# A mixture of experts in 4 chunks of 896 inner columns in place of 7 of 512

## The reference

```python
def moe_swiglu(h, w_router, w_gate, w_up, w_down):
    logits = (hf @ w_router).astype(jnp.float32)
    top_val, top_idx = lax.top_k(logits, TOP_K)      # 2 of 8
    gates = jax.nn.softmax(top_val, axis=-1)
    ...
    def expert_block(args):
        xb, e = args
        return (jax.nn.silu(xb @ w_gate[e]) * (xb @ w_up[e])) @ w_down[e]
    ...
    out = jnp.einsum('tk,tkd->td', gates.astype(y.dtype), y)
```

## Time and profile before

| | us |
|---|---|
| median of 3 runs | 2171.3 (2170.34 to 2173.81) |
| the profiled execution, its own time | 2171.86 |
| its span in the profile | 2170.1 |
| PE busy in the span | 2023.1 |
| DVE busy | 1515.5 |
| ACT busy | 1197.9 |

### The profile page before, as it was taken

The page is one execution under the profiler, slowest core; times in us unless marked ns, Lnnn a source line. Parts: engine busy times, 40 slices in busy tenths (PEclk is TensorE's granted clock), DMA queues, the critical chain, the costliest instruction groups (busy, mean ns, idle before and its releaser), DMA issues.

```text
span 2170.1 us, 22855 instructions
## 1 busy us (share of the span) xinstructions
PE 2023.1 (93%) x9571; PEld 1664.5 (77%) x9571; DVE 1515.5 (70%) x1370; ACT 1197.9 (55%) x1151; POOL 148.7 (7%) x118
## 2 busy tenths in 40 slices
PE   5999998999988799989769999999999999999995
PEld 4877776888977588867548788888888888888884
DVE  4645454444697544467558878887988888798886
ACT  5554344343643433344237667676776767677772
POOL 1301100000141200031010000000000000000000
PEclk9999998999999899989669999999999999999998
DMA  7434334444522444533139989899999989899992
GB/s 259 155 117 155 114 120 176 174 155 175 187 85 97 175 179 162 183 136 117 39 106 339 361 324 362 326 371 332 362 359 330 364 323 369 322 358 367 341 360 93
DMA packets 217661, 511.55 MB, mean 236 GB/s; under 512 B 4318, under 2 KB 8528, under 8 KB 217552
## 3 DMA queue, kind: packets, MB, share of 16 engines
q1 hardware_dynamic: 215232, 502.81, 64.3%
q0 software_dynamic: 1424, 4.59, 0.7%
q10 hardware_dynamic: 896, 2.62, 0.3%
HBM read 508.95 MB, written 1.05 MB: 235 GB/s over the span
## 4 chain that ended last, share of the span: by engine, by line
PE 85%; DVE 7%; ACT 3%; DMA 3%; issue 1%; POOL 0%; DVEq 0%; ACTq 0%; POOLq 0%
PE PS L373 25%; PE PS L374 25%; PE PS L375 25%; DVE WLB L1472 1%; DMA ring<-in_moe_w_down 1%; PE PS L846 1%; ACT WHB L994 1%; PE PS L379 1%; PE PS L393 1%; PE PS L708 1%; PE PS L798 1%; DMA ring<-in_w_mem_kv 1%; PE PS L481 1%; DVE WLX L1472 1%; DVE AR L1813 1%
## 5 line engine op out<-in xcount | busy, mean ns | idle before, releaser
L1472 DVE TENSOR_TENSOR WLB<-ring,WHB 128x2048 fp32r<-128x2048 f32 (+1 forms) x356 | 660.8, 1869 | 190.5 <-ACT WHB L994 190.2
L994 ACT ACTIVATE WHB<-ring 128x2048 fp32r<-128x2048 f32 (+1 forms) x356 | 546.4, 1540 | 408.1 <-PE PS L375 360.6
L1472 DVE TENSOR_TENSOR WLX<-ring,WHX 128x2048 fp32r<-128x2048 f32 (+1 forms) x204 | 455.3, 2244 | 76.1 <-ACT WHX L994 76.1
L994 ACT ACTIVATE WHX<-ring 128x2048 fp32r<-128x2048 f32 (+1 forms) x204 | 383.2, 1883 | 226.8 <-PE PS L375 178.9
L373 PE MATMUL PS<-WHB,XH 128*128 128x512 f32 (+1 forms) x688 | 279.3, 406 | 6.0 <-ACT LT L1033 2.9
L374 PE MATMUL PS<-WLB,XH 128*128 128x512 f32 (+1 forms) x688 | 272.6, 396 | 0.0
L375 PE MATMUL PS<-WHB,XL 128*128 128x512 f32 (+1 forms) x688 | 272.0, 395 | 0.0
L373 PE MATMUL PS<-WHB,EH 128*128 128x512 f32 x448 | 177.7, 397 | 0.0
L373 PE MATMUL PS<-WHX,EH 128*128 128x512 f32 x448 | 177.3, 396 | 0.0
L374 PE MATMUL PS<-WLB,EH 128*128 128x512 f32 x448 | 175.7, 392 | 0.0
L375 PE MATMUL PS<-WHB,EL 128*128 128x512 f32 x448 | 175.7, 392 | 0.0
(11 more groups left out here) (348 smaller groups left out, 3075.0 us busy)
## 6 DMA issues: line engine op xcount, KB each, us to landing
ring<-in_moe_w_gate SPq DMA_DIRECT2D x56, 2048.0 KB, 8.7
ring<-in_moe_w_up SPq DMA_DIRECT2D x56, 2048.0 KB, 9.8
ring<-in_moe_w_down SPq DMA_DIRECT2D x56, 2048.0 KB, 8.2
ring<-in_w_in SPq DMA_DIRECT2D x13, 2048.0 KB, 8.0
ring<-in_hg_w_in SPq DMA_DIRECT2D x8, 2048.0 KB, 8.2
ring<-in_da_w_in SPq DMA_DIRECT2D x6, 2048.0 KB, 8.0
ring<-in_w_gate SPq DMA_DIRECT2D x5, 2048.0 KB, 7.8
ring<-in_w_up SPq DMA_DIRECT2D x5, 2048.0 KB, 7.8
```

Source lines behind the costliest of these rows:

```text
L994: e.activation(hi, src, ACT.Copy).then_inc(s_hi, 1)
L1472: e.tensor_tensor(lo, src, hi.bitcast(F32), ALU.subtract).then_inc(s_lo, 1)
```

## The change

An expert is done in 4 chunks of 896 inner columns. A gate or up load is now 4 row tiles by 896 columns (runs of 3584 bytes), so there are two loads for each; a down chunk is a load of 4 and one of 3 row tiles. Pieces have 1792, 2048 or 1024 elements per partition. A product of 896 columns goes to two PSUM banks, 448 columns each: gate to banks 0 and 1, up to 2 and 3, and these are no longer alternated. A chunk's turn is 7 transposes into banks 6 and 7, and the copies L1398 and L2035 work on 896 columns at once (L1442 and L2077 of the changed file). `ring4` is a fourth slot, of the experts alone; the token copies `HH` and `HL` take the place of `XH` and `XL` to make room, so ACT waits for the router's product before it writes them. The gather is split: q = 0 ahead of the down product, q = 1 between its halves. `scatter_lists` moves from behind the up product of the sixth chunk to between the turn and the up product of the last. Two combines follow each other in chunks 1 and 2.

```diff
+CH = 896
+NCH = FFE // CH
...
+        HH, HL = (x[:, :, :].rearrange("p a n -> p (a n)").rearrange("p (t d) -> p t d", t=2) for x in (XH, XL))
...
+            EHT, ELT = (x[:, :, :].rearrange("p a n -> p (a n)") for x in (HTH, HTL))
...
+            ring4 = pt("ring4", [128, 4096])
+        P8 = ctx.enter_context(nc.psum_tensor("PS", [128, 4096], F32))
+        PS = [P8[:, 512 * b:512 * b + 512] for b in range(8)]
...
+        def half_cols(name, c0, t0):
+            return (name, (c0, t0), I[name].rearrange("(t p) n -> p t n", p=128)[:, t0:t0 + 4, c0:c0 + CH], 4, CH)
...
-        WL_M = ffn_list([(f"moe_w_gate_2.{e}", f"moe_w_up_2.{e}", f"moe_w_down_2.{e}") for e in range(NE)], FFE)
+        WL_M, held = [], []
+        for ex in range(NE):
+            for c in range(NCH):
+                for name in (f"moe_w_gate_2.{ex}", f"moe_w_up_2.{ex}"):
+                    WL_M += [half_cols(name, CH * c, 0), half_cols(name, CH * c, 4)]
+                WL_M += held
+                held = [rows(f"moe_w_down_2.{ex}", 7 * c, 7 * c + 4), rows(f"moe_w_down_2.{ex}", 7 * c + 4, 7 * c + 7)]
+        WL_M += held
...
+        SLOT = [i % NSLOT for i in range(N_PRE)]
+        for m in range(len(WL_M)):
+            SLOT.append(NSLOT if m % 4 == 3 else (N_PRE + m % 4) % NSLOT)
+        USE = [SLOT[0:i].count(SLOT[i]) for i in range(len(WL))]
+        BEFORE = [max((j for j in range(i) if SLOT[j] == SLOT[i]), default=-1) for i in range(len(WL))]
...
+            def gather(ex, q):
                 pe.wait_ge(s_po, ex + 1)
                 pe.wait_ge(s_hh, 2)
                 pe.wait_ge(s_hl, 2)
...
+                for n, src in enumerate((HH, HL)):
...
+            def expert_half(kind, name, ex, c, b0):
+
+                for q in range(4):
+                    hi, lo, used = next_piece(name, (CH * c, 4 * (q // 2)))
+                    pe.wait_ge(s_eh, 2 * ex + q // 2 + 1)
+                    pe.wait_ge(s_el, 2 * ex + q // 2 + 1)
+                    for j in range(2):
+                        kt = 2 * q + j
+                        for s in range(2):
+                            if kt == 0:
+                                room(b0 + s)
+                            cs = slice(448 * s, 448 * s + 448)
+                            t = mm3(PS[b0 + s][:, 0:448], EH[:, kt, :], EL[:, kt, :], hi[:, j, cs], lo[:, j, cs], kt == 0, kt == 7)
                     t.then_inc(used[0], 1)
-                banks.put((kind, ex, c), b, full=used, out=None if kind == "mg" else (s_h8, 7 * ex + c + 1))
+                for s in range(2):
+                    banks.put((kind, ex, c, s), b0 + s, full=used, out=(s_sgt if kind == "mg" else s_h8, NCH * ex + c + 1))
...
             def expert_turn(ex, c):
-                i = (7 * ex + c) % 2
+                n = NCH * ex + c
                 room(6)
-                pe.wait_ge(s_h8, 7 * ex + c + 1)
-                turn4(6, HID[:, i, :], ("mt", ex, c), out=(s_htl, 24 + 7 * ex + c + 1))
-
-            def expert_down(ex, c):
-                i = (7 * ex + c) % 2
-                for h2 in range(2):
-                    hi, lo, used = next_piece(f"moe_w_down_2.{ex}", 4 * c)
-                    pe.wait_ge(s_htl, 24 + 7 * ex + c + 1)
-                    if c == 0 and h2 == 0:
+                room(7)
+                pe.wait_ge(s_h8, n + 1)
+                for j in range(7):
+                    t = e.transpose(P8[:, 3072 + 128 * j:3200 + 128 * j], HID[:, n % 2, 128 * j:128 * j + 128], ident)
+                t.then_inc(banks.put(("mt", ex, c), 7, out=(s_htl, 24 + n + 1)), 1)
+                banks.put(("mt", ex, c, 6), 6, full=banks.full["mt", ex, c], out=(s_htl, 24 + n + 1))
...
+            def expert_down(ex, c, between=lambda: None):
+                n = NCH * ex + c
+                for q in range(4):
...
+                    if q == 1:
+                        between()
...
-            gather(0)
+            for q in range(2):
+                gather(0, q)
             before = None
             for ex in range(NE):
-                for c in range(7):
-                    i = (7 * ex + c) % 2
-                    expert_half("mg", f"moe_w_gate_2.{ex}", ex, c, i)
+                for c in range(NCH):
+                    last = c == NCH - 1
+                    expert_half("mg", f"moe_w_gate_2.{ex}", ex, c, 0)
                     if before is not None:
                         expert_turn(*before)
-                    expert_half("mu", f"moe_w_up_2.{ex}", ex, c, 2 + i)
-                    if c == 6 and ex < NE - 1:
-                        gather(ex + 1)
-                    if ex and 1 <= c <= 4:
-                        combine(ex - 1, c - 1)
-                    if c == 5:
+                    if last:
                         scatter_lists(ex)
+                    expert_half("mu", f"moe_w_up_2.{ex}", ex, c, 2)
+                    if ex and c in (1, 2):
+                        combine(ex - 1, 2 * c - 2, 7)
+                        combine(ex - 1, 2 * c - 1, 6)
+                    more = last and ex < NE - 1
+                    if more:
+                        gather(ex + 1, 0)
                     if before is not None:
-                        expert_down(*before)
+                        expert_down(*before, (lambda: gather(ex + 1, 1)) if more else (lambda: None))
...
+                a.wait_ge(*banks.full["rt", 0])
...
+            def expert_gate(ex, c):
+                n = NCH * ex + c
+                a.wait_ge(*banks.full["mg", ex, c, 1])
+                if n >= 2:
+                    a.wait_ge(*banks.full["mt", (n - 2) // NCH, (n - 2) % NCH])
+                if n < 2:
+                    a.wait_ge(s_most, 1)
+                g = P8[:, 0:1024].rearrange("p (s n) -> p s n", s=2)[:, :, 0:448]
+                e.activation(HID[:, n % 2, :].rearrange("p (s n) -> p s n", s=2), g, ACT.Silu).then_inc(s_sgt, 1)
 
             def expert_turned(ex, c):
-                n = 7 * ex + c
                 a.wait_ge(*banks.full["mt", ex, c])
-                if n >= 2:
-                    a.wait_ge(*T["ht read", (n - 2) // 7, (n - 2) % 7, "m"])
-                e.activation(HTH[:, n % 2, :], PS[6][:, :], ACT.Copy).then_inc(s_hth, 1)
+                e.activation(EHT[:, 0:CH], P8[:, 3072:3072 + CH], ACT.Copy).then_inc(s_hth, 1)
...
+                for c in range(NCH):
+                    pieces_done(4)
+                    expert_gate(ex, c)
                     if before is not None:
                         expert_turned(*before)
-                    pieces_done(2)
-                    if c == 6 and ex < NE - 1:
-                        gathered(ex + 1)
+                    pieces_done(4)
+                    more = c == NCH - 1 and ex < NE - 1
+                    if more:
+                        gathered(ex + 1, 0)
                     if before is not None:
                         pieces_done(2)
-                        if before[1] == 6:
+                        if more:
+                            gathered(ex + 1, 1)
+                        pieces_done(2)
...
-            row_lows(0)
...
+            row_lows(0)
             row_lows(1)
...
+                e.tensor_tensor(ELT[:, 0:CH], P8[:, 3072:3072 + CH], EHT[:, 0:CH].bitcast(F32), ALU.subtract).then_inc(s_htl, 1)
...
+                    last = c == NCH - 1
+                    pieces_done(4)
                     if before is not None:
                         expert_turned(*before)
...
                         scatter_lists(ex)
                         if ex < NE - 1:
                             lists(ex + 1)
+                    pieces_done(4)
+                    expert_up(ex, c)
+                    if ex and c in (1, 2):
+                        combined(ex - 1, 2 * c - 2, 7)
+                        combined(ex - 1, 2 * c - 1, 6)
+                    more = last and ex < NE - 1
+                    if more:
+                        gathered(ex + 1, 0)
                     if before is not None:
                         pieces_done(2)
-                        if before[1] == 6:
+                        if more:
+                            gathered(ex + 1, 1)
...
+                if BEFORE[i] >= 0:
+                    q.wait_ge(s_lo, LAST_OF[BEFORE[i]] + 1)
+                elif SLOT[i] == NSLOT:
+                    q.wait_ge(s_used, FIRST["E"])
+                e.dma_start(slot(i)[:, 0:t * n].rearrange("p (t n) -> p t n", t=t), WL[i][2]).then_inc(s_ring[SLOT[i]], 16)
...
```

More of the change, by code:

```diff
@@ L115, in build @@
         XL = sb("XL", [128, 8, S], FR)
+        HH, HL = (x[:, :, :].rearrange("p a n -> p (a n)").rearrange("p (t d) -> p t d", t=2) for x in (XH, XL))
         CT = sb("CT", [128, C_KEEP])
-        LEVM = sb("LEVM", [128, 1024], U16)
+        with ExitStack() as part:
+            LEVM = part.enter_context(nc.sbuf_tensor("LEVM", [128, 1024], U16))
+        PO = sb("PO", [128, 2, CAP], FR)
+        POT = sb("POT", [128, 2, 128], FR)
         VS = sb("VS", [128, 256])
@@ L245, in build @@
             FIRST[part_name] = len(PIECES)
```

(56 more changed lines are left out.)

82 lines of the change are left out of this document (36 added, 46 removed).

## The result

The changed kernel takes 2216.3 us (median of 4 runs, 2211.0 to 2219.5), the kernel before 2172.6 in the same comparison: ratio 1.0199, 95% interval 1.0175 to 1.0222. It is slower by 43.8 us; the forecast was 2206, range 2190 to 2222. The profiled execution took 2219.49 us.

What follows compares the result with a forecast made beforehand. The prediction took the experts as bound by PE's own instructions, not transfers: 2171.9 - 20.5 (gather) + 5.0 (matmuls) + 32 (stalls) + 17 (half clock) + 1.0 (end) = 2206.4, less 0.6 for the median, 2205.8 us; range 2190 to 2222.

Steps and rivals of the forecast that it cites:

- The move of the lists: At scatter_lists behind the transposes: PE waits for DVE's subtraction, 4.0 us at eight places, 32 us, plus 17 us half clock.
- The half clock: Behind each of eight stalls at the lists: 1.3 stretches of 3.4 us at half clock, costing 17 us.
- The gather's split: At seven gather borders: 7.7 us of idle and 12.8 us of half clock go, 20.5 us together.
- The first rival: At the gathers: 128-column matmuls themselves bring half clock, so 12.8 us stay and time is 2219 us; chance 0.10.
- a longer idle brings it without them: Argument from 3.30 us of idle before 658.72: half clock of 3.4 us follows without the gather's 128-column matmuls.
- The wide form: In gate and up: 3072 matmuls of 448 columns for 2688 of 512, 384 more at 0.013 us, add 5.0 us.
- signs of being right: On PE: about 4 us idle before the lists eight times, half clock behind, 448-column step 0.200, busy share below 0.97.
- The end: At the last turn: PE waits 2.5 us where it waited 1.5, so 1.0 us more.
- Costed at nothing: ACT and DVE pieces, single bank pairs, more loads, larger packets, fourth slot and start: nothing, or little.
- A short wait and a faster kernel: At the lists: stall and clock together under 1.8 us each; at 1 us each, 2165 us; chance 0.08.
- Transfers as the bound: Weight transfers, 0.94 busy, bind and 3584-byte runs give back at most 10 us; about 2196 us; chance 0.05.
- Wait and gain: Stalls of 2.4 us each and less half clock cancel against the gain and 10 us from packets; near 2173; chance 0.04.

Runs made afterwards that it cites:

- lists_mid: Changed kernel with scatter_lists moved between the two halves of the last up product instead of ahead of it; 2164.1 us, 0.9965 of before.
- split_only: Kernel before, 7 chunks of 512, with only the gather split around the down product; 2150.1 us, 0.9902 of before.
- lists_mid_narrow: lists_mid with each gate and up load issued as two transfers of 448 columns, runs of 1792 bytes; 2163.8 us, 0.9969 of before.
- act_first: Changed kernel with Silu and the copy of the transposes ahead of the weight piece on ScalarE; 2194.9 us, 1.0113 of before.
- lists_mid_slots3: lists_mid with the experts' loads in three slots again, ring4 unused; 2191.6 us, 1.0078 of before.
- widths: Changed kernel with the 896 gate and up columns cut in 512 + 384 instead of 448 + 448; 2217.7 us, 1.0219 of before.
- lists_mid_pitch: lists_mid with columns cut in 512 + 384 and split rows laid 1024 elements apart; 2163.3 us, 0.9959 of before.
- lists_mid_sfirst: lists_mid with the loops inside a piece exchanged, six matmuls on one PSUM bank instead of three; 2165.8 us, 0.9973 of before.

## Why the prediction was right, point by point

**The move of the lists**, priced at 32 + 17 us, cost 52.2 (lists_mid). The stall was 3.76 us for a forecast of 4.0 (30.1 us, 32.0 by the weight loads, which wait first), in the place, with the releaser and in the order of the chain that was forecast: from the end of the gate product (1355.41) to the end of the subtraction (1360.04) the rows above have 4.63 us, for 4.6 forecast. Taking the piece out of the chain moved it by what the piece costs. The half clock is the term mis-sized: I took 1.3 stretches of 3.4 us for each stall; there were 15 in 8, 1.9 each, 51 us, in which a 448-column matmul steps by 0.373 for 0.205: 23 us, or 22 without the 2.8 us that fell into the idle time. The earlier trace rows had one stretch behind 3.30 us and two behind 4.1 and more; 3.76 us mostly went with the second.

**The gather's split**, priced at 20.5 us, gave 22.0 alone. That the half clock would go with the idle time, which I only took as so, is shown by split_only and lists_mid: same matmuls, clock 1.00. The first rival falls. One argument against it was misread, though: "a longer idle brings it without them" doesn't hold, since the row at 658.72 in the earlier trace rows is itself a group of 128-column matmuls. That the rival fell is owed to these two runs and not to that row.

**The wide form.** I had 5.0 us for 384 more matmuls. From the starts at full clock between 1140 and 2140 us, 448 columns step by 0.2051 us on average and the 512 of gate and up before by 0.2296: 3072 x 0.2051 - 2688 x 0.2296 = 12.9 us. A chain of the changed kernel shows where:

```profile
1399.92 0.21 PE PS L399
...
1404.88 0.21 PE PS L399
```

24 steps of 0.2067, the commonest value, which is 448 / 2.4 GHz (0.1867) and 0.020, where the earlier trace rows have 0.2133 and 0.014. On average the part beside the columns is 0.0184 us against 0.0163 before. So the term was mis-sized, 12.9 for 5.0: the straight line through 256 and 512 is too low for the new form. lists_mid, which is free of stalls until the last turn, is still 14 us behind split_only, and this is most of it. What makes the fixed part larger isn't settled; the number 448, the address of the weights and the change of bank are excluded. The forecast also named 0.200 for this step and a PE busy share below 0.97 as signs of being right: they came out at 0.205 and 0.971, both missed.

**The end.** PE waited 3.36 us for the last turn, for 2.5 forecast and 1.5 before:

```profile
2177.31 2.86 ACT L1031 ACTIVATE WHX<-ring 128x2048 fp32r<-128x2048 f32 x2 [0.86 <-PE PS L401]
...
2178.42 0.93 PE L898 MATMUL PS<-CT,HID 128*128 128x128 f32 x7
2179.26 2.29 DVE L1515 TENSOR_TENSOR WLX<-ring,WHX 128x2048 fp32r<-128x2048 f32 x1 [0.48 <-ACT WHX L1031]
2180.08 0.90 ACT L1442 ACTIVATE HTH<-PS 128x896 fp32r<-128x896 f32 x1
2181.47 1.08 DVE L2077 TENSOR_TENSOR HTL<-PS,HTH 128x896 fp32r<-128x896 f32 x1
```

ACT's copy started 1.66 us behind the turn where I had 1.16, since it stood behind two pieces in a row, and DVE's subtraction another 0.5 us late behind a low part of 2.29 us, which I had left out. The stretch of 3.4 us at half clock began with PE's restart and cost about 1.6 us. The start cost nothing that can be told.

**Costed at nothing.** Right for the packets (lists_mid_narrow) and for the pieces on ACT and DVE, whose busy times grew by 5.3 and 0.1 us. Wrong in its reasoning for the fourth slot: it is what lets the smaller loads be free; without it they cost some 25 us. I judged the slot by the row that PE never waits for a piece, and that row held for the old loads in the old slots. The total wasn't hurt by this only because the slot is part of the change, which is luck.

**The other rivals.** A short wait and a faster kernel: 3.76 us against the threshold of 1.8 for stall and clock together; act_first has 2.18 and one stretch and is slower still, as that threshold says. Transfers as the bound: no, their busy share fell to 0.89 and PE waited for no piece. Wait and gain didn't cancel.

**The sum.** Differences between the runs give - 22.0 (split) + 52.2 (lists) + 14.0 (wide form with the end) = 44.2 for 43.8, but these three must add up, since each run is subtracted from the next; only the kernel before was measured anew in between. Parts that are read from the rows are a check: - 22.0 + 30.1 (stalls) + 22 (half clock behind them) + 12.9 (steps) + 1.9 (longer wait at the end) + 1.6 (half clock there) = 46.5 for 43.8. The 2.7 us between them aren't placed. The forecast was 10 us too low: half clock (17 for 22), the steps (5.0 for 12.9) and the end (1.0 for 3.5) were all priced too low, the stalls 2 us too high.

## What to carry to other kernels

A few small matmuls that are moved along an in-order queue take their wait with them: before moving them, follow the semaphore of the bank they write to, and count the whole chain on the other engines up to it. On a TensorE that is otherwise full, a stall can cost itself and a half clock behind it, here 3.76 us of idle and about 2.8 of clock, and then shortening it pays more than its length; but the clock isn't sure to fall (2 stretches behind 17 idle times in lists_mid_slots3), so read it from the trace. Split a change into its parts: here the split of the gather alone makes the kernel before 1% faster, while the whole rewrite with the split in it gives at best 0.4%.

## What the runs showed that I had not expected

- The time at half clock behind a stall was 3.4 or 6.8 us, and the idle time sets it only loosely. Idle of 0.75 us: four times 3.4, once 6.8, once none. 2.18 us: 3.4 in eight of eight places. 3.76 us: 6.8 in seven of eight, and in six of eight in widths. The wait of 3.4 us at the last turn, the same in seven kernels: none in act_first, 3.4 in the changed kernel and lists_mid_pitch, 6.8 in the other four (widths, lists_mid, lists_mid_sfirst, lists_mid_narrow).
- In lists_mid_slots3 the 12 waits for a piece (up to 1.39 us, with 448-column matmuls behind them) brought no half clock before the next stall; the two stretches there follow waits ahead of the lists.
- A matmul's cost beside its columns isn't a constant. On average, at full clock: 0.0163 us for the 512 columns of gate and up before, 0.0184 for 448, and 0.020 and 0.016 for 512 and 384 in turn.
- Removing one of four slots, with TensorE never waiting for weights before, cost some 25 us.
